# The DeltaNet gates' projection in native float32, in four column groups of the array, ahead of each input tile's other products

## The reference, cut to what matters

```python
def gdn_mixer(x, w_in, conv_w, a_log, dt_bias, norm_g, w_out):
    h = x @ w_in
    qkv, z, b_raw, a_raw = jnp.split(h, [...], axis=-1)      # b_raw, a_raw: (B, S, 8) each
    ...
    beta = jax.nn.sigmoid(b_raw)
    g = -jnp.exp(a_log) * jax.nn.softplus(a_raw + dt_bias)
    o = gated_delta_rule(q, k, v, beta, g)
```

## Time and profile before

| | before |
|---|---|
| device time, median of 3 runs | 1701.24 us (1699.92 to 1701.26) |
| profiled execution, its own time | 1697.84 us |
| its span, first to last instruction | 1696.1 us |
| mean granted TensorE clock | 0.999 |
| PE busy | 1657.9 us (98%), 11176 products |
| DVE, ACT, POOL busy | 944.2, 811.5, 277.4 us (56%, 48%, 16%) |

### The profile page before, as it was taken

How to read it: one execution, slowest core, us unless ns; L and a number is a source line. 1 busy time by engine, 2 the same in 40 slices (tenths; PEclk the granted TensorE clock), 3 DMA queues, 4 the chain that set the end, 5 groups by cost and what they waited for, 6 DMA issues and landing times. The chain is left out here.

```text
span 1696.1 us, 28865 instructions
## 1 busy us (share of the span) xinstructions
PE 1657.9 (98%) x11176; PEld 1269.5 (75%) x11176; DVE 944.2 (56%) x1729; ACT 811.5 (48%) x1308; POOL 277.4 (16%) x240
## 2 busy tenths in 40 slices
PE   9999999999999989999999999999999999999998
PEld 6777777787777768878888788666666666678887
DVE  5747566675757553974374272354444544559633
ACT  4737455574746562242233342656556655642411
POOL 5213122221212131000000001222212221300000
PEclk9999999999999999999999999999999999999999
DMA  6211020311101031241122023111111111232311
GB/s 159 59 37 38 26 51 14 51 36 41 39 26 39 26 125 29 87 150 40 47 77 72 13 63 76 40 44 34 48 32 44 32 32 35 79 118 90 121 47 53
DMA packets 119943, 96.26 MB, mean 57 GB/s; under 512 B 19904, under 2 KB 103552, under 8 KB 119808
## 3 DMA queue, kind: packets, MB, share of 16 engines
q1 hardware_dynamic: 119808, 94.43, 19.7%
HBM read 85.92 MB, written 8.49 MB: 56 GB/s over the span
## 5 line engine op out<-in xcount | busy, mean ns | idle before, releaser
L467 PE MATMUL gdn_unit<-part_hi,weights_hi 128*128 128x512 f32 x496 | 225.5, 455 | 0.0
L469 PE MATMUL gdn_unit<-part_hi,weights_lo 128*128 128x512 f32 x496 | 195.3, 394 | 0.0
L468 PE MATMUL gdn_unit<-part_lo,weights_hi 128*128 128x512 f32 x496 | 193.9, 391 | 0.0
L2677 DVE CUSTOM_DVE_ANT_0 fa_probs<-fa_scores,fa_decay 128x896 f32<-128x896 f32 (+7 forms) x128 | 97.1, 758 | 118.7 <-PE fa_scores L2464 71.4
L909 DVE SCALAR_TENSOR_TENSOR x<-gdn_raw,gdn_taps,x 128x512 f32<-128x512 f32 x144 | 129.3, 898 | 23.9 <-ACT x L706 19.0
L2614 ACT ACTIVATE fa_probs_t<-fa_turned 128x512 f32<-128x512 f32 (+1 forms) x96 | 52.3, 545 | 140.2 <-PE fa_turned L2481 139.7
L430 POOL TENSOR_TENSOR weights_lo<-ring,weights_hi 128x1024 fp32r<-128x1024 f32 x31 | 75.2, 2425 | 250.6 <-ACT weights_hi L686 250.6
L469 PEld LDWEIGHTS gdn_unit<-part_hi,weights_lo 128*128 128x128 f32 x496 | 93.1, 188 | 20.9
L2593 ACT ACTIVATE fa_probs<-fa_probs,fa_top 128x896 f32<-128x896 f32 (+7 forms) x128 | 99.4, 777 | 18.3 <-DVE fa_top L2677 14.6
L1391 PE MATMUL e_gate<-e_w_hi,part_hi 128*128 128x512 f32 (+1 forms) x272 | 104.7, 385 | 2.0 <-DVE e_w_lo L1611 1.2
L467 PEld LDWEIGHTS gdn_unit<-part_hi,weights_hi 128*128 128x128 f32 x496 | 93.7, 189 | 15.9 <-issue 3.6
(11 more groups left out here) (396 smaller groups left out, 3736.6 us busy)
## 6 DMA issues: line engine op xcount, KB each, us to landing
ring<-in_gdn_w_in_dram SPq DMA_DIRECT2D x31, 512.0 KB, 4.1
ring<-in_fox_w_in_dram SPq DMA_DIRECT2D x20, 512.0 KB, 4.7
fa_decay<-c_rows_scratch SPq DMA_DIRECT2D x64, 128.0 KB, 3.0
e_more_raw<-in_ple_w_gate_dram SPq DMA_DIRECT2D x18, 256.0 KB, 5.3
gdn_g_bc<-g_rows_scratch SPq DMA_DIRECT2D x8, 512.0 KB, 8.6
ring<-in_fox_w_in_dram SPq DMA_DIRECT2D x16, 256.0 KB, 2.8
ring<-in_fox_w_out_dram SPq DMA_DIRECT2D x16, 256.0 KB, 3.5
m_old<-x_scratch SPq DMA_DIRECT2D x8, 512.0 KB, 3.5
```

The costliest lines, as they stand in the source:

```text
L467: pe.matmul(out, w_hi[:, j % 2, k, :], xh[:, k, ts], start=(k == 0), stop=False)
L468: pe.matmul(out, w_hi[:, j % 2, k, :], xl[:, k, ts], start=False, stop=False)
L469: mm = pe.matmul(out, w_lo[:, j % 2, k, :], xh[:, k, ts], start=False, stop=(k == KT - 1))
L2677: step(dve.tensor_tensor_reduce(probs[:, n % 3, blocks(e)], scores[head][:, blocks(e)], decay[:, head, blocks(e)], 1.0, 3e38, ALU.add, ALU ...
```

## The change

The split of the gate columns goes, with its semaphores, on ACT and on DVE. PE multiplies the raw gate columns with the raw input tile in native float32. The 1024 tokens are four quarters of 256, and the products of quarter `q` are written to partitions 32q to 32q+15 of `w2`, in its first 256 columns: each quarter has its own group of 32 columns of the array. They stand ahead of the six products of the same tile and wait for the loads alone. ACT copies the four quarters with four instructions, and PE's transposes wait for all four.

```diff
+QUARTERS = 4
+QUARTER_T, QUARTER_P = T // QUARTERS, P // QUARTERS
+def quarter(q):
+    return slice(q * QUARTER_T, (q + 1) * QUARTER_T)
+def quarter_rows(bank, q, rows):
+    return bank[q * QUARTER_P:q * QUARTER_P + rows, 0:QUARTER_T]
...
                 for k in range(KT):
                     if k == 0:
+                        pe.wait_ge(ab_loaded, 16)
+                    pe.wait_ge(x_loaded[k], 16)
+                    for q in range(QUARTERS):
+                        mm = pe.matmul(quarter_rows(w2, q, 2 * H), ab_raw[:, k], x_raw(k)[:, quarter(q)],
+                                       start=(k == 0), stop=(k == KT - 1))
+                    if k == KT - 1:
+                        mm.then_inc(ab_product, 1)
+                    if k == 0:
                         pe.wait_ge(early_low, 1)
...
-                    if k == 0:
-                        pe.wait_ge(gate_low, 1)
-                    for half in range(2):
-                        out, ts = w2[0:2 * H, half * HALF:(half + 1) * HALF], slice(half * HALF, (half + 1) * HALF)
-                        pe.matmul(out, ab_hi[:, k], xh[:, k, ts], start=(k == 0), stop=False)
-                        pe.matmul(out, ab_hi[:, k], xl[:, k, ts], start=False, stop=False)
-                        mm = pe.matmul(out, ab_lo[:, k], xh[:, k, ts], start=False, stop=(k == KT - 1))
-                mm.then_inc(ab_product, 1)
...
-                    pe.wait_ge(ab_copied, 1)
+                    pe.wait_ge(ab_copied, QUARTERS)
...
-                    step(act.activation(ab_rows, w2[0:2 * H], ACT.Copy), ab_copied)
+                    for q in range(QUARTERS):
+                        step(act.activation(ab_rows[:, quarter(q)], quarter_rows(w2, q, 2 * H), ACT.Copy), ab_copied)
...
-                    act.wait_ge(ab_loaded, 16)
-                    step(act.activation(ab_hi, ab_raw, ACT.Copy), gate_high)
...
-                    dve.wait_ge(gate_high, 1)
-                    step(dve.tensor_tensor(ab_lo, ab_raw, ab_hi.bitcast(F32), ALU.subtract), gate_low)
```

More of the change, by code:

```diff
@@ L246, in delta_net @@
         ab_raw = o_t[:, 1, 0:KT * 2 * H].rearrange("p (k h) -> p k h", k=KT)
-        ab_hi, ab_lo = sb("ab_hi", [P, KT, 2 * H], F32R)[:], sb("ab_lo", [P, KT, 2 * H], F32R)[:]
         work = [by_head(o_t[:, 2, n * NT * H:(n + 1) * NT * H]) for n in range(6)]
@@ L277, in delta_net @@
         ds_made, s_made, o_made, o_taken = sem("ds_made"), sem("s_made"), sem("o_made"), sem("o_taken")
-        gate_loaded, gate_high, gate_low = sem("gate_loaded"), sem("gate_high"), sem("gate_low")
+        gate_loaded = sem("gate_loaded")
         ab_product, ab_copied, ab_turned = sem("ab_product"), sem("ab_copied"), sem("ab_turned")
```

## The result

| | before | changed |
|---|---|---|
| device time, median of 20 runs | 1700.35 us (1697.55 to 1701.26) | 1704.15 us (1698.74 to 1706.54) |
| ratio, 95% interval | | 1.0023 [1.0016, 1.0030] |
| profiled execution | 1697.84 us (span 1696.1) | 1703.88 us (span 1701.9) |
| mean granted TensorE clock in it | 0.999 | 0.993 |

The changed kernel is slower by 0.23%, 3.8 us, where the forecast had 0.5 us. The time lies within the range, near its upper end, and just beyond the 0.2% that I called no change.

What follows compares the result with a forecast made beforehand. PE (busy 1657.9 of 1696.1 us) bounds the kernel, but the taps' chain holds L467 until 30.56, so 5.2 us less PE work saves nothing. Half clock behind the gap adds 0.5 us: 1701.7 us, range 1698.8 to 1704.6.

Steps and rivals of the forecast that it cites:

- What ends last at 30 us: End of the first products: L467 can't start before 30.56, held by the taps' chain; 5.2 us less PE work saves nothing.
- The price of the new products: First products: the gates cost 0.73 us a tile (0.43 to 1.01) instead of 1.38, ending at 25.4 (23.0 to 27.6).
- Rival (b): First products: column groups don't run abreast, 3.4 us a tile, gates' chain 6.9 us late, 1708.1 us; chance 0.07.
- The four copies on ACT: Gate rows: four copies take 1.7 us, 0.7 more, yet end 0.16 us earlier, useful only if PE is on time.
- The gap and the clock: Ahead of L467: PE idles 5.2 us (3.0 to 7.6), then half clock for some 3.4 us; gates' chain 0.5 late.
- rival (a): Behind the gap: the clock stays up and everything after is 0.16 us early, 1701.1 us; chance 0.15.
- From 52 us on every record stands 0.5 us later: After the gates' arithmetic: PE is full until the last head, so the 0.5 us shift goes on to the end.
- Rival (c), PE's work counts after all: First stage: small loads land 5 us earlier, so the whole 5.2 us are saved, 1696.0 us; chance 0.03.
- The chances: Whole kernel: faster 0.04, same 0.88, slower 0.08, with no change meaning within 0.2% (3.4 us).

Runs made afterwards that it cites:

- before with a gap: The kernel before with the gates' products of input tiles 1 to 4 left out (wrong sums), against the kernel before: 1702.60 us, ratio 1.0013 [1.0004, 1.0022].

## Why the prediction was right or wrong

- *What ends last at 30 us*: right. With the gates cheaper L478 still waited for POOL's low part behind the taps, and the 5 us of PE work taken out there saved nothing.
- *The price of the new products*: right. 0.77 us a tile (2.15 less the 1.38 of six other products) against 0.73 forecast, an end at 25.5 against 25.4. Rival (b) is refuted by the run with one column group; its own price, 6.9 us, came out as 7.3 at 50 us and 8.7 between the medians (1710.51 against 1701.83 of the kernel before beside it). The Trainium skill, "TensorE: Matmul & The Clock Gate", section "Step-by-step: what each phase is for", says that the bus of the last quarter isn't supported. These records don't bear that out: all four products are done in 0.56 us, so the fourth group runs as the others do.
- *The four copies on ACT*: right, 1.60 us for four against 1.7, and worth nothing, since PE was late.
- *The gap and the clock*: the mechanism was right, and rival (a), the clock stays up, didn't come in any of four profiles with this gap (three of the changed kernel, one of before with a gap). The term that was too small is its length. I took the 3.4 us of half clock of the earlier trace rows and allowed 5; measured were 6.8, 10.2, 3.4 and, in before with a gap, 10.2. I took one case for the size. What sets the length wasn't shown. In the profile with 3.4 us PE was 0.2 us behind at 50 us, but its small loads had landed 0.3 us earlier than in before (26.56 against 26.87). With these differences taken off, my estimate of the shift is 0.5 us for 3.4 us of half clock, which is the forecast, 1.1 for 6.8, and 1.8 and 2.2 for 10.2. Where it lasted 3.4 us, PE still waited 0.79 us for the gates' arithmetic at 50 us (forecast: under 0.8); in the other three that wait is gone, and PE's own lateness ends last, which the sum had hidden behind the gates' chain.
- *"From 52 us on every record stands 0.5 us later"*: wrong, and the second step that failed. I took the full PE up to 590 us as proof that a shift is passed on and didn't ask what runs beside it. L441 met L954, and PE waited 1.44 us; behind 600 more half clock came. The row for the meeting was in the trace of before: the first L946 of that head took 2.50 us beside POOL's L452, the others 0.42. The Trainium skill, "SBUF — State Buffer", in its table of terms, says that DVE and GpSimd share a pair of ports that one of them holds for a whole instruction while the other is blocked; the trace agrees, since L954 took what was left of L441 (2.27 us) and 0.28 more. What moved the two together is only in part shown: none of the six profiles with full clock from 25 to 50 us has the meeting, four of the six with half clock there have it, and the two others (3.4 and 10.2 us) don't, so the length doesn't decide it.
- *Rival (c), PE's work counts after all*: not in this change. It does once the taps' chain and the wait for the copied rows are gone: -4.5 us at 50 us with the taps by one DMA and DVE's copies.
- *The chances*: 0.92 on no change or faster was too much. I had priced the spread of the clock from three runs. The fall that I expected there has a price of its own in each execution, and its upper end should have been read as a chance of slower, not as a tail. That the measured time lies in the range is luck in part: the difference is +3.8 us and not +0.5, and the range was laid around a median of three runs, 1701.24, that lay 0.9 us above the median of twenty. Laid around 1700.35 it would have ended at 1703.7, below the 1704.15 measured.

## What to carry to other kernels

When two things end together at one place, a cheaper one of the two only opens a gap. Ask what the gap does to the clock before asking what it saves: here 5 us of PE work less were 3.8 us more, and filling the gap with useless products was worth 0.15%. The saving came out clear of noise only when the other chain went too, and with it one of the two waits that had taken its place.

## What the runs showed of the hardware that I had not expected

- At gaps of 3.7 to 5.4 us the clock stood at the 1.2 GHz level for 3.4, 6.8, 10.2 and 10.2 us, though PE had work again all that time but for the last 1.8 us of the gap at most.
- Two waits of 0.86 and 1.35 us, 3 us apart, were followed by 3.4 us of half clock, in two kernels; 0.86 us alone and 1.6 us alone weren't. Nor were two of 2.35 and 1.36 us, as far apart, in a third kernel, so no rule for short waits comes out of these runs.
- Four native float32 products of 128x16 by 128x256 on four column groups take 0.56 us up to the next work, the same four on one group 1.83 us.
- A DVE operation of 0.42 us took 2.55 us beside a POOL operation of 2.37 us that had started 0.1 us earlier.
- Four loads of 12 KB in 4-byte pieces kept SP's queue for 9.1 to 10.6 us, and for 14.8 us issued ahead of the gate vectors; one load of the same 48 KB in rows of 512 bytes, 1.6 to 1.8 us.
